# The residual stream brought from feature order to token order for the last projection, by another route

## The reference

```python
for i in range(DEPTH):
    ...
    h = h + mix.astype(h.dtype)
    h = h + conv_glu_ffn(rms_norm(h, norm_ffn[i]), ffn_w_up[i], ffn_conv[i], ffn_w_down[i]).astype(h.dtype)
return rms_norm(h, final_norm)
```

## Time and profile before

| | |
|---|---|
| three runs | 2337.62 us median (2337.58 to 2337.98) |
| the profiled execution | 2337.73 us |
| its span | 2335.9 us |
| busy | TensorE 2326.5, VectorE 1688.5, ScalarE 1049.3 us |
| DMA | 434.88 MB, mean 186 GB/s |

### The profile page before, as it was taken

One profiled execution on the slowest core, in us unless ns is written; L12 is line 12 of the kernel. 1 busy time (PEld: TensorE's weight loads), 2 busy tenths in 40 slices (PEclk: granted clock), 3 DMA queues, 4 the chain that ended last, 5 costly groups with the idle time before them and its releaser, 6 DMA issues.

```text
span 2335.9 us, 36790 instructions
## 1 busy us (share of the span) xinstructions
PE 2326.5 (100%) x12892; PEld 2034.3 (87%) x12892; DVE 1688.5 (72%) x2139; ACT 1049.3 (45%) x1157; POOL 2.7 (0%) x8
## 2 busy tenths in 40 slices
PE   9999999999999999999999999999999999999998
PEld 8988888888888888888888888888888888888887
DVE  7978788768788788765555676766788788785544
ACT  7344443554444444434444444444444444443443
POOL 0000000000000000000000000000000000000000
PEclk9999999999999999999999999999999999999999
DMA  7555555565656656666665656565655656666665
GB/s 250 159 170 164 163 177 158 175 196 181 192 179 197 189 180 197 185 198 191 190 191 182 194 185 192 186 194 174 201 181 188 198 180 190 194 203 185 193 191 158
DMA packets 388490, 434.88 MB, mean 186 GB/s; under 512 B 13361, under 2 KB 341425, under 8 KB 388273
## 3 DMA queue, kind: packets, MB, share of 16 engines
q1 hardware_dynamic: 387392, 431.26, 59.7%
q10 hardware_dynamic: 1008, 2.43, 0.3%
HBM read 431.54 MB, written 2.10 MB: 186 GB/s over the span
## 4 chain that ended last, share of the span: by engine, by line
PE 99%; DMA 0%; DVE 0%; ACT 0%; issue 0%; SPq 0%; ACTq 0%
PE acc L1147 47%; PE acc L1157 25%; PE acc L1192 7%; PE acc L1194 7%; PE acc L1193 7%; PE acc L1170 3%; PE acc L1179 1%; PE side L1320 1%; PE side L1299 0%; PE side L1315 0%; PE side L1125 0%; DMA raw<-in_hgrn_w_in 0%; PE side L1137 0%; DVE xn L661 0%; ACT h L546 0%; DVE w_parts L603 0%
## 5 line engine op out<-in xcount | busy, mean ns | idle before, releaser
L603 DVE TENSOR_TENSOR w_parts<-raw,w_parts 128x1024 fp32r<-128x1024 f32 x816 | 983.2, 1223 | 584.8 <-PE acc L1157 310.3
L352 ACT ACTIVATE w_parts<-raw 128x1024 fp32r<-128x1024 f32 x815 | 856.2, 1058 | 1007.3 <-PE acc L1147 639.8
L1147 PE MATMUL acc<-xn,w_parts 128*128 128x512 f32 x4352 | 1040.3, 391 | 0.8 <-DVE xn L661 0.8
L1147 PEld LDWEIGHTS acc<-xn,w_parts 128*128 128x128 f32 x4352 | 799.4, 188 | 156.2 <-DVE xn L661 1.4
L1157 PEld LDWEIGHTS acc<-xn,w_parts 128*128 128x128 f32 x4352 | 557.4, 191 | 20.7 <-DVE w_parts L603 0.4
L1157 PE MATMUL acc<-xn,w_parts 128*128 128x256 f32 x4352 | 567.0, 283 | 0.0
L1192 PE MATMUL acc<-w_parts,act 128*128 128x512 f32 x704 | 274.5, 390 | 0.0
L1194 PE MATMUL acc<-w_parts,act 128*128 128x512 f32 x704 | 273.9, 389 | 0.0
L1193 PE MATMUL acc<-w_parts,act 128*128 128x512 f32 x704 | 273.9, 389 | 0.0
L1194 PEld LDWEIGHTS acc<-w_parts,act 128*128 128x128 f32 x704 | 132.1, 188 | 27.6
L1193 PEld LDWEIGHTS acc<-w_parts,act 128*128 128x128 f32 x704 | 132.2, 188 | 27.2
(11 more groups left out here) (130 smaller groups left out, 998.6 us busy)
## 6 DMA issues: line engine op xcount, KB each, us to landing
raw<-in_ffn_w_up SPq DMA_DIRECT2D x352, 512.0 KB, 3.6
raw<-in_ffn_w_down SPq DMA_DIRECT2D x176, 512.0 KB, 4.7
raw<-in_hgrn_w_in SPq DMA_DIRECT2D x127, 512.0 KB, 3.9
raw<-in_sc_w_in SPq DMA_DIRECT2D x96, 512.0 KB, 4.6
raw<-in_hgrn_w_out SPq DMA_DIRECT2D x32, 512.0 KB, 4.2
raw<-in_sc_w_out SPq DMA_DIRECT2D x32, 512.0 KB, 4.4
h<-in_x SPq DMA_DIRECT2D x3, 512.0 KB, 8.6
final_w<-in_final_norm ACTq DMA_DIRECT2D x1, 1024.0 KB, 7.2
```

What stands on the lines that cost most here:

```text
L352: nc.scalar.activation(w_parts[:, c % RING, :, 0, :], raw[:, c % RING], ACT.Copy).then_inc(hi_ready, 1)
L603: v.tensor_tensor(w_parts[:, c % RING, :, 1, :], raw[:, c % RING], w_parts[:, c % RING, :, 0, :].bitcast(F32), ALU.subtract).then_inc(lo_r ...
L1147: o = mm(to[:, j, :], w[:, q, 0, j * P:(j + 1) * P], src[:, k * KW + q, :, :].rearrange("p n t -> p (n t)"), start=begin and q == 0, stop= ...
```

## The change

TensorE's transposes and VectorE's copies go. In their place VectorE makes four 32x32-block transposes of 128x1024 elements at steps 5, 6, 12 and 15 of its own program, into ta and tb in turn. A block transpose leaves features of one quarter of the partitions in that quarter. So SP then issues 64 transfers of 32 partitions x 2 x 128 elements (32 KB), four in each of the steps 14 to 29, from partition quarter a of ta or tb to quarter q of h_tok, ahead of the weight load of that step. The features of a group of 512 come to lie in the order (quarter, tile, feature) in h_tok, and the sums and products read them through the rearranged views by_feature and features. The sum of the last group goes straight to y_tok. VectorE gets waits: at steps 12 and 15 for the transfers that read ta and tb before, at the end of the first group for all 64.

```diff
--- before.py
+++ after.py
@@ -124,7 +124,9 @@
 S_DOWN = S_RS_UP0 + 1
 S_RS_SC = S_DOWN + DT // TG
 S_RS_UP1, S_H = S_RS_SC + 1, S_RS_SC + 2
-TURN_H_AT = [6, 9, 12, 15]
+QUARTER = P // 4
+TURN_H_AT = [5, 6, 12, 15]
+MOVE_H_AT = [14, 18, 22, 26]
 
 
 def loop(e, phase, body, peel_last=False):
@@ -246,6 +248,7 @@
         qk_ready = sem("qk_ready")
         final_w_loaded = sem("final_w_loaded")
         h_turned = sem("h_turned")
+        h_moved = [sem(f"h_moved{n}") for n in range(2)]
         sum_ready = sem("sum_ready")
         sq_tok_ready = sem("sq_tok_ready")
         first_block_done = sem("first_block_done")
@@ -257,6 +260,14 @@
         y_stored = sem("y_stored")
 
         sums = tb[:].rearrange("p j t -> p (j t)").rearrange("p (b n) -> p b n", b=T // P)
+        def by_feature(t):
+
+            return t.rearrange("p (a j f) -> p j a f", a=4, f=QUARTER)
+
+        def features(t):
+
+            return t.rearrange("p (j a f) -> p j a f", a=4, f=QUARTER)
+
         y_tok = h[:].rearrange("p j t -> p (j t)").rearrange("p (b n) -> p b n", b=T // P)
 
         block = ctx.enter_context(nc.Block())
@@ -283,6 +294,15 @@
 
         @block.sync
         def _(sp):
+            def move_h(m, a):
+
+                src = [ta, tb][m % 2][a * QUARTER:(a + 1) * QUARTER].rearrange("p j t -> p (j t)") \
+                    .rearrange("p (b q n) -> p b q n", q=4, n=P)
+                first = m * GC + a * P
+                for q in range(4):
+                    sp.dma_start(h_tok[q * QUARTER:(q + 1) * QUARTER, :, first:first + P], src[:, :, q, :]) \
+                        .then_inc(h_moved[m % 2], 16)
+
             def stream(phase, w, column):
 
                 def body(i, first):
@@ -296,6 +316,13 @@
 
                             sp.wait_ge(lo_ready, at(i, phase.cpi, c + 1))
                             sp.sem_inc(loads_begun, 1)
+                            if first and phase is DOWN1:
+                                for m, begin in enumerate(MOVE_H_AT):
+                                    a = g * phase.cpg + kk - begin
+                                    if a == 0:
+                                        sp.wait_ge(h_turned, m + 1)
+                                    if 0 <= a < 4:
+                                        move_h(m, a)
                             if first and c == 0:
                                 load_first(rows_of(phase, w, k, part, column(i, g)))
                                 continue
@@ -532,7 +559,7 @@
 
                 act_e.wait_ge(sum_ready, n * (T // P) + b + 1)
                 nc.scalar.activation(ta[:, 2 * b:2 * b + 2, :].rearrange("p j t -> p (j t)"),
-                                     h_tok[:, b, n * GC:(n + 1) * GC], ACT.Square,
+                                     (y_tok if n == DT // TG - 1 else h_tok)[:, b, n * GC:(n + 1) * GC], ACT.Square,
                                      accum_out=sq_tok[:, n, b:b + 1]).then_inc(sq_tok_ready, 1)
 
             def finish(b):
@@ -1052,14 +1079,14 @@
                 cols = slice(n * GC, (n + 1) * GC)
                 if first:
                     carry(g, kk)
-                if first and g == 0 and kk - 1 in TURN_H_AT:
-                    m = TURN_H_AT.index(kk - 1)
-                    dve.wait_ge(stage_done, S_H + m + 1)
-                    v.tensor_copy(h_tok[:, :, m * GC:(m + 1) * GC],
-                                  side[:, (S_H + m) % STAGES].rearrange("p (b n) -> p b n", b=T // P)) \
-                        .then_inc(h_turned, 1)
-                    dve.wait_ge(h_turned, m + 1)
-                    v.sem_inc(stage_free, 1)
+                if first and g == 0 and kk in TURN_H_AT:
+                    m = TURN_H_AT.index(kk)
+                    if m == 1:
+                        dve.wait_ge(act_ready, 2 * (DT // TG) + UP0.n + UP1.n)
+                    if m >= 2:
+                        dve.wait_ge(h_moved[m % 2], 16 * 16)
+                    v.transpose([ta, tb][m % 2][:].rearrange("p j t -> p (j t)"),
+                                h[:, m * TG:(m + 1) * TG, :].rearrange("p j (b n) -> p b j n", n=QUARTER)).then_inc(h_turned, 1)
                 if (n, kk) == (DT // TG - 1, RING):
 
                     dve.wait_ge(sq_tok_ready, n * (T // P))
@@ -1073,6 +1100,9 @@
                         finish(n, g, b, cols)
                     return
                 dve.wait_ge(hi_used, DOWN1.c0 + (n + 1) * DOWN1.cpg + RING)
+                if n == 0:
+                    for moved in h_moved:
+                        dve.wait_ge(moved, 16 * 16 * 2)
                 for b in range(T // P):
                     add_down(g, b, cols)
                 if n == 0:
@@ -1081,12 +1111,14 @@
                     dve.wait_ge(sum_ready, n * (T // P) + b + 1)
                     if b == T // P - 1:
                         v.sem_inc(acc_free, 1)
-                    v.tensor_tensor(y_tok[:, b, cols], h_tok[:, b, cols], final_w[:, cols], ALU.mult) \
+                    v.tensor_tensor(features(y_tok[:, b, cols]), by_feature(h_tok[:, b, cols]), features(final_w[:, cols]),
+                                    ALU.mult) \
                         .then_inc(y_ready, 1)
 
             def add_down(g, b, cols):
 
-                v.tensor_tensor(h_tok[:, b, cols], h_tok[:, b, cols], acc[:, g % SETS, b, :], ALU.add) \
+                v.tensor_tensor(by_feature(h_tok[:, b, cols]), by_feature(h_tok[:, b, cols]), features(acc[:, g % SETS, b, :]),
+                                ALU.add) \
                     .then_inc(sum_ready, 1)
 
             def finish(n, g, b, cols):
@@ -1095,7 +1127,8 @@
                     dve.wait_ge(first_block_done, 1)
                 else:
                     dve.wait_ge(hi_used, CHUNKS + RING)
-                add_down(g, b, cols)
+                v.tensor_tensor(features(y_tok[:, b, cols]), by_feature(h_tok[:, b, cols]),
+                                features(acc[:, g % SETS, b, :]), ALU.add).then_inc(sum_ready, 1)
                 dve.wait_ge(sq_tok_ready, n * (T // P) + b + 1)
                 v.scalar_tensor_tensor(out=std[:, b:b + 1], in0=sq_tok[:, n, b:b + 1], scalar=1.0 / D,
                                        in1=sq_part[:, b:b + 1], op0=ALU.mult, op1=ALU.add).then_inc(var_ready, 1)
@@ -1105,7 +1138,7 @@
                 dve.wait_ge(y_ready, n * (T // P))
                 y = y_tok[:, b, 2 * GC:3 * GC]
                 v.tensor_scalar(y, y, rs[:, b:b + 1], None, ALU.mult).then_inc(y_tok_ready, 1)
-                v.scalar_tensor_tensor(out=y_tok[:, b, cols], in0=h_tok[:, b, cols], scalar=rs[:, b:b + 1],
+                v.scalar_tensor_tensor(out=y_tok[:, b, cols], in0=y_tok[:, b, cols], scalar=rs[:, b:b + 1],
                                        in1=final_w[:, cols], op0=ALU.mult, op1=ALU.mult).then_inc(y_last_ready, 1)
 
             phase_of(DOWN1, final, True)
@@ -1347,16 +1380,7 @@
             phase_of(SC_OUT, act, act_ready, G + UP0.n)
             phase_of(UP1, xn, xn_ready, 6 * G, 2, (4, S_RS_UP1))
 
-            def turn_h(g, kk):
-
-                if g == 0 and kk in TURN_H_AT:
-                    n = TURN_H_AT.index(kk)
-                    pe.wait_ge(ident_loaded, 16)
-                    pe.wait_ge(h_ready, 6 * G)
-                    stage(S_H + n, [turn(h[:, n * TG + j, b * P:(b + 1) * P], (b * TG + j) * P)
-                                    for b in range(T // P) for j in range(TG)])
-
-            phase_of(DOWN1, act, act_ready, 2 * G + UP0.n, carry=turn_h)
+            phase_of(DOWN1, act, act_ready, 2 * G + UP0.n)
 
 
 _WEIGHTS = ["hgrn_w_in", "hgrn_w_out", "sc_w_in", "sc_w_out", "ffn_w_up", "ffn_w_down", "final_norm"]
```

## The result

Before 2337.82 us, after 2346.24 us (medians of six runs each, 2337.58 to 2338.36 and 2345.61 to 2347.39): ratio 1.0036, 95% interval 1.0026 to 1.0046. The forecast was 2334.2, the range ended at 2337.4. The profiled execution took 2347.39 us, its span is 2345.6, 9.7 more than before. Of all executions behind this document one fell out of line: one of the 21 of experiment 5's kernel took 4349 us at a granted clock of 0.83; it was not seen again, nothing here explains it, and it is left out of the ratios.

What follows compares the result with a forecast made beforehand. TensorE's unbroken row of matmuls was taken to bound the kernel. Removed transposes, -3.6 us, and a stall of 0.2 us at chunk 26 took the median from 2337.62 to 2334.2 us; range 2333.4 to 2337.4 us.

Steps and rivals of the forecast that it cites:

- the one on SP's queue: SP, steps 14 to 29: five issues at 0.368 us take 1.84 of 2.72 us, each weight load issued 1.47 us later.
- Cover: Weight load of chunk 29: 9.3 us to spare before TensorE needs it, so 1.47 us of later issue is hidden.
- The wait at step 21: End of first column group: VectorE waits for all 64 transfers; stall taken as 0.2 us, between 0 and 3.2 us.
- S - 4.0: TensorE's stall at chunk 26 in us: time to the last transfer's landing, less the cover.
- S: Time from the end of VectorE's split of chunk 25 to the last transfer's landing: 4.2 to 7.2 us, taken as 4.2.
- Rival 2: Steps 14 to 29: transfers fill the DMA rings and a backlog eats the gain; slower, up to 2350.0 or 2359 us; chance 0.10.
- the prediction's two prices: Ring time per transfer within on-chip memory: 0.11 us if paid by bytes, 0.23 us if paid by packets.
- Rival 1: Step 21: last transfers land late and the wait costs TensorE 0.8 to 3.2 us, 2334.9 to 2337.3 us; chance 0.20.
- Rivals 3 and 4: VectorE's transposes take 7.0 us each, 2339.5 us, chance 0.04; TensorE's removed transposes return full duration, 2328.9 us, chance 0.04.
- VectorE's transposes: Four 32x32-block transposes on VectorE: 1.2 us each, hidden in its idle time, costing nothing on the path.
- 3.6 us for 32 transposes: TensorE, last projection: removing 32 transposes, all on the path, gains 3.6 us by chunk distances, not 8.8 by recorded durations.
- DMA share under 1: Steps 14 to 29: the 64 transfers lift DMA engine share from 0.61 to between 0.77 and 0.95, so hidden.

Runs made afterwards that it cites:

- experiment 5: Changed kernel with three transfers per step on SP in steps 14 to 35, per-block waits, later transposes, squares to a free buffer: 2334.09 us, again 2334.18 us.
- experiment 9: Changed kernel with the 64 transfers reading the same shapes from input x in device memory instead of ta and tb: 2335.86 us, ratio 0.9991.
- experiment 2: Changed kernel with VectorE's wait for the transfers of blocks 1 and 3 moved to the end of the second column group: 2336.15 us, ratio 0.9994.
- experiment 6: Changed kernel with two of each four transfers issued by ScalarE in its steps 6 to 21, the others by SP: 2334.86 us, ratio 0.9987.

## Why the prediction was wrong

**The step that failed** is the one on SP's queue: "One issue takes 0.368 us, so five take 1.84 us of 2.72". The row was that of a load from device memory that stands alone, one per 2.72 us. Between transfers within on-chip memory an issue takes 0.64 us with its distance to the next, and a step of five 3.25 us. The step had the right question (issues per step against the chunk's time) and took its price from a row with another source and other neighbours: the neighbours raise it to 0.43 at most, the source to 0.59 (experiment 9). I gave the other new costs a bound from each side, and this one, which decided, a single value.

**Cover.** "That leaves 9.3 us, so 1.47 us more is hidden" was worked out for the load of chunk 29, which has no other work behind it. The tight place is chunk 25: its split ended 8.3 us ahead of TensorE's want, and the adds, the squares and the next split take 4.2 of them, which leaves 4.1 for lag and wait together. Late loads took 5.3 (3.0 us ahead instead of 8.3), and that alone cost a gap of 1.3 us in experiment 2. The wait draws on the same cover, and the transfers it waits for stand at the end of the lagging queue.

**The wait at step 21** was named as the tight one, and its formula S - 4.0 held to 0.2 us in experiments 6 and 9 and, with the 5.3 us of late loads added, for the change itself. Its size was off: S was 8.6, outside my 4.2 to 7.2, because SP had not reached step 29 when the split of chunk 25 ended. Without lag it was 5.4 (experiment 9, read from device memory) and 4.5 (experiment 6), where I had taken 4.2.

**Rival 2** had the form of what happened, a rate against the chunk's time with a backlog that eats its cover, but in the wrong place: rings instead of the issuing queue. A part of its sign came true all the same, ScalarE waiting for loads, since a late issue and a slow ring look alike from there; the landing time, 4.6 us as before, tells them apart. The Trainium skill ("DMA: Bandwidth & Descriptors", Bandwidth) gives 0.68 us at 4 KB and 0.95 us at 64 KB, for loads from device memory. These transfers within on-chip memory take much less of the engines than that: GpSimd's 64 raised the DMA share from 0.58 to 0.86 for 36 us, by my estimate 0.28 x 36 / 64 = 0.16 us each, between the prediction's two prices of 0.11 and 0.23. No chance of mine stood for SP's queue, and to count rival 2's 0.10 for it would be luck. Rival 1's mechanism is what remains in the versions without lag that keep all waits at step 21 (gaps of 0.6 and 1.6 us). Rivals 3 and 4 are refuted: VectorE's transposes take 1.24 us each, and the floor is 3.3 to 3.6 us under the kernel before, not 8.7.

**What held**: 3.6 us for 32 transposes (3.3 to 3.6 measured), read from the distances and not from durations; VectorE's transposes (1.2 taken, 1.24 measured), the strided sums (682 taken, 680 to 688 ns) and the end of the kernel at nothing (7.9 us from the last matmul's start to the end of the span, before and after); DMA share under 1. Experiment 5 lands on the forecast, 2334.1 against 2334.2 us, but it has no wait for all 64 transfers at step 21. With that wait and no lag (experiment 9) it is 2335.9 us: inside the range, and 1.7 above the forecast.

**Not in the sum**: the low clock behind a long gap. It turned 10.0 us of standstill into 12.8.

## What to carry to other kernels

Price the issue of a transfer by a row with the same source, the same target and the same neighbours, and count a queue's issues per step against the step: a queue just over its budget loses a little each step, and shows it only where something waits for its end. Small transfers that aren't urgent belong on an idle engine's queue or spread until the queue's step fits. Where a new wait and a lagging queue share one cover, add them before comparing with it, and add the low clock when the gap is long: here gaps up to 1.6 us left it alone, and those from 7.7 us on cost 2.4 us and more on top.

## What was not expected of the hardware

An issue on SP takes 0.37 us for a lone load from device memory, 0.40 to 0.43 in a row of five such, 0.33 us for a store from on-chip to device memory, and 0.59 to 0.62 when source and target are both on-chip memory, with the same for a load directly behind it, even with an eighth of the data. ScalarE's queue shows the same 0.6 at the same time, GpSimd's 0.53. TensorE's clock fell early in a standstill of 10 us (at about 2158.4, the last matmul having ended at 2156.55) and was at 0.50 for the first 6 us behind it.
